# Leading slabs in eighths of the reduction, feed-forward columns by one reduction each, and three weight units without a w_ada product

## The reference

```python
mod = jax.nn.silu(c) @ w_ada + b_ada                       # 1024 x 6144
shift_m, scale_m, gate_m, shift_f, scale_f, gate_f = jnp.split(mod, 6, axis=-1)
h = rmsnorm(x, g_mix_pre) * (1.0 + scale_m[:, None]) + shift_m[:, None]
z = h @ w_in
q, k, v, fl, pu, ch, cb, cc, gl = jnp.split(z, cuts, axis=-1)
br_a = forgetting_attention(q, k, v, fl + b_f)             # softmax with a cumulated log-sigmoid of fl
...                                                        # pool mixer, short conv, gates, w_branch, w_out
x = x + gate_m[:, None] * rmsnorm(y, g_mix_post)
h2 = rmsnorm(x, g_ff_pre) * (1.0 + scale_f[:, None]) + shift_f[:, None]
y2 = jnp.square(jax.nn.relu(h2 @ w_ff1)) @ w_ff2
return x + gate_f[:, None] * rmsnorm(y2, g_ff_post)
```

## Time and profile before

| | |
|---|---|
| profiled execution | 767.74 us |
| span of its trace | 766.5 us |
| other executions | 768.32, 768.35, 767.16 us |
| PE busy | 756.8 us, 99% |
| DVE busy | 580.8 us, 76% |
| ACT busy | 447.5 us, 58% |
| POOL busy | 73.3 us, 10% |
| first product with weights | starts 14.03 us after the span's start |
| units 0 to 15 | 14.03 to 61.56 us |
| last matmul ends | about 761.3 us |

### The profile page before, as it was taken

How to read it: one execution, slowest core, us unless ns; L and a number is a source line. 1 busy time by engine, 2 the same in 40 slices (tenths; PEclk the granted TensorE clock), 3 DMA queues, 4 the chain that set the end, 5 groups by cost and what they waited for, 6 DMA issues and landing times.

```text
span 766.5 us, 11109 instructions
## 1 busy us (share of the span) xinstructions
PE 756.8 (99%) x4276; PEld 651.1 (85%) x4276; DVE 580.8 (76%) x808; ACT 447.5 (58%) x673; POOL 73.3 (10%) x128
## 2 busy tenths in 40 slices
PE   8999999999999999999999999999999999999997
PEld 6998877888898888888899997789988888888885
DVE  5989999989796576776787998667758755665664
ACT  7666687775664444444474497467547644444453
POOL 5035720000200000000020001110001100000000
PEclk9999999999999999999999999999999999999999
DMA  9989998655477776866556554446434766666641
GB/s 355 398 280 353 329 346 306 229 184 163 139 222 217 243 239 208 281 189 198 184 169 214 167 164 149 147 161 206 146 99 138 219 194 193 192 192 192 189 168 55
DMA packets 77751, 161.29 MB, mean 210 GB/s; under 512 B 5170, under 2 KB 7538, under 8 KB 77699
## 3 DMA queue, kind: packets, MB, share of 16 engines
q1 hardware_dynamic: 76272, 157.31, 62.6%
q10 hardware_dynamic: 994, 2.79, 1.0%
q0 software_dynamic: 432, 0.49, 0.2%
HBM read 159.51 MB, written 1.05 MB: 209 GB/s over the span
## 4 chain that ended last, share of the span: by engine, by line
PE 94%; DVE 3%; ACT 2%; issue 1%; DMA 0%; DVEq 0%; ACTq 0%
PE bank L2058 18%; PE bank L2059 17%; PE bank L2060 17%; PE bank L2160 15%; PE bank L2163 8%; PE bank L2134 5%; PE bank L2071 2%; PE bank L2078 2%; PE bank L2073 2%; PE bank L2518 1%; PE bank L2091 1%; PE bank L2213 1%; PE bank L2334 1%; DVE lo_ring L1123 1%; PE bank L2258 1%
## 5 line engine op out<-in xcount | busy, mean ns | idle before, releaser
L1123 DVE TENSOR_TENSOR lo_ring<-raw_ring,hi_ring 128x1024 fp32r<-128x1024 f32 x247 | 302.6, 1231 | 135.7 <-ACT hi_ring L567 134.8
L567 ACT CAST hi_ring<-raw_ring 128x1024 fp32r<-128x1024 f32 x247 | 258.5, 1052 | 233.0 <-PE bank L2060 128.3
L2058 PE MATMUL bank<-hi_ring,branch_hi 128*128 128x512 f32 x352 | 138.5, 394 | 0.0
L2059 PE MATMUL bank<-lo_ring,branch_hi 128*128 128x512 f32 x352 | 137.2, 390 | 0.0
L2060 PE MATMUL bank<-hi_ring,branch_lo 128*128 128x512 f32 x352 | 137.0, 389 | 0.0
L2160 PE MATMUL bank<-h_hi_lo,hi_ring 128*128 128x512 f32 x512 | 128.1, 392 | 0.0
L2160 PEld LDWEIGHTS bank<-h_hi_lo,hi_ring 128*128 128x128 f32 x512 | 92.9, 189 | 17.2
L2060 PEld LDWEIGHTS bank<-hi_ring,branch_lo 128*128 128x128 f32 x352 | 66.1, 188 | 14.1
L2058 PEld LDWEIGHTS bank<-hi_ring,branch_hi 128*128 128x128 f32 x352 | 66.1, 188 | 13.9 <-issue 0.9
L2059 PEld LDWEIGHTS bank<-lo_ring,branch_hi 128*128 128x128 f32 x352 | 66.2, 188 | 13.0 <-issue 0.2
L2163 PEld LDWEIGHTS bank<-h_hi_lo,lo_ring 128*128 128x128 f32 x512 | 69.8, 190 | 5.0
(11 more groups left out here) (341 smaller groups left out, 1162.8 us busy)
## 6 DMA issues: line engine op xcount, KB each, us to landing
raw_ring<-in_w_ff SPq DMA_DIRECT2D x128, 512.0 KB, 3.7
raw_ring<-in_w_in SPq DMA_DIRECT2D x63, 512.0 KB, 4.5
raw_ring<-in_w_out SPq DMA_DIRECT2D x16, 512.0 KB, 3.3
raw_ring<-in_w_xkv SPq DMA_DIRECT2D x16, 512.0 KB, 3.6
mem_v<-in_w_ada SPq DMA_DIRECT2D x13, 512.0 KB, 5.0
mem_k<-in_w_ada SPq DMA_DIRECT2D x11, 512.0 KB, 5.2
ada_ring<-in_w_ada SPq DMA_DIRECT2D x8, 512.0 KB, 7.3
raw_ring<-in_w_branch SPq DMA_DIRECT2D x8, 512.0 KB, 3.4
```

What stands on the lines that cost most here:

```text
L567: act.copy(m.hi[:, m.slot(u)], m.raw[:, m.slot(u)]).then_inc(s.hi_done, 1)
L1123: dve.tensor_tensor(m.lo[:, m.slot(u)], m.raw[:, m.slot(u)], as_f32(m.hi[:, m.slot(u)]), ALU.subtract).then_inc(s.lo_done, 1)
L2058: pe.matmul(out, a_hi, b_hi, start=start, stop=False, skip_group_check=True)
L2059: pe.matmul(out, a_hi, b_lo, start=False, stop=False, skip_group_check=True)
```

## The change

The change has three parts.

1. **Leading slabs by eighths.** Unit 2k now holds the q and k columns of the 128 rows of chunk k, unit 2k+1 their v and mixer columns. All four slabs accumulate in PSUM over k = 0 to 7 (q in banks 0 and 1, k in 2 and 3, v in 4 and 5, mixer in 6 and 7). The additions of V are gone, the copies of q, k, v and mixer out of PSUM come when each slab is complete, and the forget logits stand behind all 16 units. The host packs c as 128 x 32 (`c_blocks`); ACT takes its silu, and two DVE transposes of a broadcast operand make the row silu(c) on all partitions, in place of the matmuls of `spread_c` and two ACT passes of 128 x 1024. Both sums of squares of x are ACT's, one reciprocal root for each tile of 128 tokens is POOL's, and the transposes go tile by tile. SP issues x, two w_ada units, unit 0, and then weight and w_ada units in turn. `cumulative` on PE moves from step 1 to step 2 of `attention1`, DVE's `cum_log_f` from step 1 to step 3.
2. **Feed-forward columns.** w_ada units 24 to 39 now come transposed too, and each is one instruction of the kind of L1142 that leaves a finished column. `fold_columns`, `folded_columns`, two of the `ada_turn` and two of the `ada_sum` are gone; one small product (`ff_scale`) is added.
3. **Three units without a w_ada product.** The products stand beside the units of the list `ADA_EARLY`: 20 to 25, 27 to 30, 32 and 34 to 46.

```diff
-V_FIRST_BANK = 3
-ADA_FIRST, ADA_LATE, ADA_UNITS, ADA_RING, ADA_UNIT = 16, 40, 48, 6, 20
-FIRST_SLABS = (2, 0, 1, 3)
+X_BANKS = (7, 6, 5, 4)
+X_COPIES = (2, 3, 1)
+ADA_FIRST, ADA_COLS, ADA_LATE, ADA_UNITS, ADA_RING, ADA_UNIT = 16, 24, 40, 48, 6, 20
+
+
+ADA_EARLY = [u for u in range(ADA_UNIT, ADA_UNIT + 27) if u - ADA_UNIT not in (6, 11, 13)]
...
 def ada_at(a):
 
-    return ADA_UNIT + a - ADA_FIRST if a < ADA_LATE else FF1 + 24 + 16 * ((a - ADA_LATE) // 4) + 2 * ((a - ADA_LATE) % 4)
+    return ADA_EARLY[a - ADA_FIRST] if a < ADA_LATE else FF1 + 24 + 16 * ((a - ADA_LATE) // 4) + 2 * ((a - ADA_LATE) % 4)
...
     units = []
     w_in = t["w_in"][0]
-    columns = (0, UN, 2 * UN, 3 * NH * DH + NH)
-    units += [unit(w_in, j * UK * P, columns[i]) for j in range(RING) for i in FIRST_SLABS]
+    for k in range(KD):
+        rows = w_in[bass.ds(k * P, P), :]
+        units += [rows[:, c:c + 2 * w].rearrange("p (a n) -> p a n", n=w)[:, :, 0:UN]
+                  for c, w in ((0, UN), (2 * UN, UN + NH))]
...
-    k, c = (a - ADA_FIRST) % KD, 2 * D + (a - ADA_FIRST) // KD * D
+    if ADA_COLS <= a < ADA_LATE:
+        return t["w_ada_T"][bass.ds(2 * D + (a - ADA_COLS) * P, P), :]
...
-    for a in range(RING):
-        load_ada(a)
+    load_ada(0)
+    load_ada(1)
     for k in range(UK):
         sp.dma_start(m.raw[:, 0, k, :], units[0][:, k, :]).then_inc(s.raw_in[0] if k else s.raw_first, DMA)
-    for q in range(RING - 1):
-        u, a = RING * q, RING * q + RING
-        load(u + 1)
-        load(u + 2)
-        load_ada(a)
-        load_ada(a + 1)
-        load(u + 3)
-        load_ada(a + 2)
-        load_ada(a + 3)
-        load(u + 4)
-    for u in range(ADA_FIRST - RING + 1, UNITS):
+    for u in range(2 * KD):
+        if u:
+            load(u)
+        if u + 2 < ADA_FIRST:
+            load_ada(u + 2)
+    for u in range(2 * KD, UNITS):
...
+    act.dma_start(m.silu_block[:, :], t["c_blocks"]).then_inc(s.rows_in, DMA)
...
+    act.wait_ge(s.rows_in, DMA)
+    act.activation(m.silu_block[:, :], m.silu_block[:, :], ACT.Silu).then_inc(s.silu_ok, 1)
+    for tt in range(NT):
+        act.wait_ge(s.x_in[tt], DMA)
+        square_sum(s.xm, tt, m.x)
+    for tt in range(NT):
+        act.wait_ge(*s.xm.rstd.at(tt + 1))
+        for n in range(2):
+            cs = slice(n * UN, n * UN + UN)
             act.activation(m.norm[:, tt, cs], m.x[:, tt, cs], ACT.Copy,
                            scale=stat[:, 4 + tt:5 + tt]).then_inc(s.xm.normed.sem, 1)
 
...
-    for u in range(10, 13):
-        after(u)
-    take_half(14, 0, pair(m.qT, 0), s.q_out)
+    after(12)
+    take_half(15, 0, pair(m.qT, 0), s.q_out)
+    take_half(15, 2, pair(m.kT, 0), s.k_out)
+    act.wait_ge(s.v_ps, 1)
+    act.copy(m.v_tok[:, 0, :], bank[4][:, :]).then_inc(s.v_out, 1)
+    take_half(16, 6, pair(mix, 0), s.mixA_out)
     after(13)
...
     act.wait_ge(s.fl_ps, 1)
     act.copy(m.fl_part, bank[4][FL_LO:FL_LO + 2 * NH, 0:S]).then_inc(s.fl_sum, 1)
     after(14)
     act.wait_ge(s.fl_neg, 1)
     own.then(act.activation(m.fl_exp, m.fl_exp, ACT.Exp))
     act.activation(m.fl_exp, m.fl_exp, ACT.Ln, bias=1.0).then_inc(s.fl_ln, 1)
-    take_half(16, 6, pair(mix, 0), s.mixA_out)
...
+        if a < ADA_FIRST or ADA_COLS <= a < ADA_LATE:
+
+            if a < ADA_FIRST:
+                k, at, shift = a // 2, (KD if a % 2 == 0 else 0) + a // 2, a % 2
+            else:
+                k, at, shift = a % KD, 2 * KD + a - ADA_COLS, a < ADA_COLS + KD
+            layer = int(a >= ADA_FIRST)
+            c = B_ADA + 3 * layer * KD + k
+            dve.tensor_tensor_reduce(out=w, in0=w, in1=m.silu_ps if a < 2 else m.silu_row, scale=1.0,
+                                     scalar=cols[:, c:c + 1] if shift else m.scale_1[:, layer, k:k + 1],
+                                     op0=ALU.mult, op1=ALU.add,
+                                     accum_out=m.adacol[:, at:at + 1]).then_inc(s.ada_used, 1)
+            return
...
+    dve.wait_ge(s.silu_ok, 1)
+    for dst in (m.silu_ps, m.silu_row):
+        own.then(dve.transpose(dst.rearrange("p (j c) -> p j c", c=BLOCK),
+                               m.silu_block[:, :].unsqueeze(2).to_broadcast([P, BLOCK, BLOCK])))
     dve.wait_ge(s.cols_in, DMA)
-    own.then(dve.tensor_scalar(m.scale_1[:, :], cols[:, B_ADA + KD:B_ADA + 2 * KD], 1.0, None, ALU.add))
-    for k in range(UK):
-        ada()
-        ada()
-        mix_columns(k)
-    lo_first(0)
+    b_ada = cols[:, B_ADA:B_ADA + 6 * KD].rearrange("p (a b k) -> p a b k", a=2, k=KD)
+    own.then(dve.tensor_scalar(m.scale_1[:, :, :], b_ada[:, :, 1, :], 1.0, None, ALU.add))
+    ada()
+    mix_columns(0)
+    ada()
+    lo_half(0, 0)
     shifted_lo(s.xm, 0)
...
-    shifted_lo(s.xm, 1)
-    lo(1)
-    dve.wait_ge(s.silu_ok, 3)
-    for q in range(RING - 1):
-        u = RING * q
-        lo(u + 2)
-        for k in (UK * q + 2, UK * q + 3):
+    lo_half(0, 1)
+    ada()
+    lo_half(1, 0)
+    lo_half(1, 1)
+    mix_columns(1)
+    ada()
+    for k in range(1, KD):
+        lo(2 * k)
+        shifted_lo(s.xm, k)
+        if k < KD - 1:
             ada()
+        lo(2 * k + 1)
+        if k < KD - 1:
+            mix_columns(k + 1)
             ada()
-            mix_columns(k)
-            if k % 2 == 0:
-                lo(u + 3)
-        shifted_lo(s.xm, UK * q + 2)
-        lo(u + 4)
-        shifted_lo(s.xm, UK * q + 3)
-        lo(u + 5)
...
+    take_half(15, 1, pair(m.qT, 2), s.q_out)
+    take_half(15, 3, pair(m.kT, 2), s.k_out)
+    dve.wait_ge(s.v_ps, 1)
+    dve.tensor_copy(m.v_tok[:, 1, :], bank[5][:, :]).then_inc(s.v_out, 1)
     after(12)
-    take_half(14, 1, pair(m.qT, 2), s.q_out)
+    take_half(16, 7, pair(mix, 2), s.mixA_out)
     after(13)
-    take_half(15, 3, pair(m.kT, 2), s.k_out)
-
...
     after(14)
-    take_half(16, 7, pair(mix, 2), s.mixA_out)
...
     own.then(dve.tensor_tensor_scan(m.cum_plain, m.fl_relu, m.fl_exp, 0.0, ALU.add, ALU.add))
@@ -1410,7 +1382,7 @@
     after(15)
 
     def attention1(step):
-        if step == 1:
+        if step == 3:
             dve.wait_ge(s.cum_ps, 1)
             dve.tensor_scalar(m.cum8[:, :, :].rearrange("p a h -> p (a h)"), bank[6][:, 0:2 * NH], -1.0, None,
                               ALU.mult).then_inc(s.cum_out, 1)
...
     for j in range(RING):
+        attention1(j)
         if j == RING - 1:
             add_parts(s.mixB_part, MIX_B_BANKS, mix[:, 4:8], s.mixB_out)
-        attention1(j)
         after(MIX_B + j)
...
-            ada_turn(FF_SCALE)
-    dve.wait_ge(s.ff_cols_ps, 1)
-    folded_columns(FOLD_BANK, 0, 16, 24)
-    folded_columns(FOLD_BANK, BLOCK, 24, 32, G_FF)
+            ff_scale()
...
+    def queries_keys(u, k):
+
+        (q_hi, q_low, q_x), (k_hi, k_low, k_x) = (feature_passes(u, i, k, 2 * i) for i in range(UK))
+        if k == 0:
+            claim(0, 1)
+            q_hi()
+            q_low()
+            q_x()
+            claim(2, 3)
+            k_hi()
+            k_x()
+            k_low().then_inc(s.used, 1)
+            return
+        q_hi()
+        k_hi()
+        q_low()
+        k_low()
+        q_x()
+        k_x().then_inc(s.used, 1)
...
+    def values_mixer(u, k):
+
+        slot, outs = m.slot(u), (bank[4][:, :], bank[5][:, :])
...
+        pe.wait_ge(*ready(s.hi_done, s.hi_first, u, 0))
+        part(m.h_hi, m.hi, start=k == 0)
+        part(m.h_lo, m.hi)
+        pe.wait_ge(*ready(s.lo_done, s.lo_first, u, 0))
+        mm = part(m.h_hi, m.lo, stop=k == KD - 1)
+        if k == KD - 1:
+            mm.then_inc(s.v_ps, 1)
+        if k == 0:
+            claim(6, 7)
+        rounded, low_weights, low_features = feature_passes(u, 1, k, 6)
+        rounded()
+        low_features()
+        low_weights().then_inc(s.used, 1)
...
     def run_up(n):
 
         for _ in range(n):
-            pe.matmul(bank[5][:, 0:S], m.ones[:, :], m.x[:, 0, 0:S], start=True, stop=True)
...
+            pe.matmul(bank[0][:, 0:P], m.ones[:, :], m.ones[:, :], start=True, stop=True)
...
+    pe.wait_ge(s.ones_ok, 1)
+    run_up(13)
     turn_first()
     run_up(4)
...
+    for k in range(KD):
+        queries_keys(2 * k, k)
+        values_mixer(2 * k + 1, k)
+    free[0] = free[1] = s.q_out, 2
     free[2] = free[3] = s.k_out, 2
+    free[4] = free[5] = s.v_out, 2
+    forget_logits()
     free[6] = free[7] = s.mixA_out, 2
...
-    def fold_columns():
-
-        b = FOLD_BANK
-        claim(b)
-        ada_fold(FF_SHIFT, bank[b][:, 0:BLOCK])
-        ada_fold(FF_SCALE, bank[b][:, BLOCK:2 * BLOCK]).then_inc(s.ff_cols_ps, 1)
-        free[b] = s.ff_cols, 2
-
     def attention1(step):
-        if step == 1:
+        if step == 2:
             cumulative()
...
             mm = tile_of(tt, OUT + RING + j, UK * j, m.h_hi, m.h_lo, OUT_BANKS[1][0], j == 0, j == RING - 1)
-            if (tt, j) == (0, 1):
-                fold_columns()
```

288 lines of the change are left out of this document (94 added, 194 removed).

## The result

The changed kernel took 769.54 us (median of 7 executions, 769.07 to 772.13) against 768.32 us before (median of 7, 766.89 to 768.57). The ratio, taken from all executions, is 1.0022, 95% interval 1.0012 to 1.0031 (that of the two medians alone is 1.0016): slower by a fifth of a percent, where the prediction had said no change. The time itself lies in the predicted range, 1.3 us above the forecast, and under the 769.9 us from which the prediction would have called it slower; it is the interval that excludes no change. The profiled execution took 769.54 us with a span of 768.3, which is 1.8 us more than the one before.

What follows compares the result with a forecast made beforehand. PE, busy 99% of the span, was taken to bound the kernel. Terms -2.4 + 3.8 - 0.4 - 0.8 = +0.2 us gave 768.2 us; the forecast's own range was 766.5 to 769.1, the wider range 765.5 to 770.4.

Steps and rivals of the forecast that it cites:

- The start: Start to unit 16: first product at 11.6 us instead of 14.03, gain kept through the 16 leading units, -2.4 us.
- The wait at unit 20: Unit 20 waits for DVE's later copy out of bank 6: 2.7 to 4.0 us, taken as +3.8.
- the three operations: On DVE ahead of that copy: w_ada product, rest of unit 22, another product; 3.8 us undisturbed, 4.9 beside POOL.
- both causes that the text named: For unit 20's wait: forget logits behind unit 15 instead of ahead, and DVE's copy moved from step 1 to 3.
- The folding: Feed-forward columns near 193 us: PE's folding work of 0.36 us goes, -0.4 us.
- The wait at 127 us: PE's 0.64 us wait for DVE's rests goes with its tail, -0.8 us; rival that it stays: 769.0, chance 0.12.
- The three products: w_ada products of skipped units 26, 31 and 33 move to units 44 to 46, where DVE idles; no term.
- The falling clock: Rival, chance 0.07: PE's clock falls in unit 20's wait of 3.8 to 4 us, costing 2 us: 770.2.
- The low clock at the start: Rival, chance 0.13: PE's clock still low when the products start, 2.8 us lost over chunk 0: 771.0.

Runs made afterwards that it cites:

- the two steps moved alone: Kernel before, with only `cumulative` at step 2 on PE and DVE's copy out of bank 6 at step 3, ahead of the mixer sums: 771.59 us, ratio 1.0038.
- Without the skip: Changed kernel with the 24 w_ada products beside units 20 to 43, no unit skipped: 769.01 us, ratio 1.0008.
- the early copy: Changed kernel with DVE's copy out of bank 6 at step 2 instead of step 3: 769.11 us, ratio 1.0008.
- the early rest: Changed kernel with the last rest of the attention ahead of the rest and w_ada product of unit 46 in DVE's queue: 767.02 us, ratio 0.9989.
- the early copy and the products at units 47 to 49: Changed kernel with the copy out of bank 6 one step earlier and the three products beside units 47 to 49 instead of 44 to 46: 767.97 us, ratio 0.9990.
- one matmul in the run-up: Changed kernel with the early copy and the early rest, and one run-up matmul instead of 13 ahead of the transposes: 766.20 us, ratio 0.9972.
- the kernel without the last run-up: Changed kernel with the early copy and the early rest, without the four run-up matmuls between transposes and unit 0: 765.37 us, ratio 0.9960.
- Two exchanges of order: Changed kernel with the early copy and the early rest together: 765.22 us, ratio 0.9959.

## Why the prediction was wrong, step by step

**The start, forecast -2.4 us, measured -2.23.** Right. The first product came at 11.44 us (forecast 11.6). Chunk 0 lasted 6.07 us where the chunks behind it last 5.7; of these 0.4 us 0.15 are PE standing for chunk 1 of h, which ACT made late because it had waited for DVE's w_ada product until 16.77 us. From there to unit 16 the pace was kept; no wait on `hi_ring`, `lo_ring` or `ada_cols` above 0.2 us showed.

**The wait at unit 20, forecast +3.8 us, measured +2.62 (2.50 of it waiting).** Mechanism, line and releaser were right and the size was off, just under the 2.7 to 4.0 that the text gave. With S the start of unit 16, DVE came to the rest of unit 19 at S + 7.1 us (forecast 7.2) and to the three operations at S + 10.5 (forecast 10.7). The step that was mis-sized is the price of the three operations ahead of the copy: I took 4.9 us because POOL works in the same stretch, and they took 3.5. POOL did work there, from 66.27 us on, so the step from "POOL is under way" to "DVE is slow" is what failed here; the last section shows who was slow instead. The wait has both causes that the text named: with the copy one step earlier it is gone, and with the logits as early as before it would be about 0.8 us, by the estimate from the two steps moved alone. One reading is off, and nothing hung on it: when unit 20 began before, at 73.17 us, DVE had the whole second product ahead of it (from 73.63 us) and not half of it.

**The folding, forecast -0.4 us, measured -0.43 over the whole stretch behind unit 44.** Right as far as this stretch can tell; not tried alone.

**The wait at 127 us, forecast -0.8 us, measured -0.63.** Right. Without the skip it was there again (0.84 us), so this term belongs to the skip. Which engine PE stood for there stays open: the views name none ("issue"), before and without the skip.

**The three products, forecast nothing.** This is the step that failed: "moves three products of 1.3 to 1.8 us to units 44 to 46, where DVE has idle time". DVE did have idle time there, 1.32 us ahead of the rest at 155.83 us in the trace of before. But the idle time came *behind* the last rest of the attention and the products went *ahead* of it. I had looked at what DVE's queue has in total and not at the one operation in it that PE was about to ask for. The order on DVE would have shown it, as it had shown the copy out of bank 6: the rest L1296 behind two rests and two products. The reversal alone (last rest ahead of unit 46) took the wait away.

The sum was +0.2 us and the trace gave +1.8: 1.2 us less than forecast at unit 20, 2.5 us more at unit 44, and small terms (+0.2 each at the start and at 127 us). Two errors of opposite sign, and so luck, brought the time within 1.3 us of the forecast; that nothing would change was wrong.

**The falling clock** was a rival with 0.07, put at a wait of 4 us and at 2 us of price. The price was about right: between the two kinds of executions lie 1.97 us with the early copy (where only one stayed up), 1.7 with the early rest and 1.3 with the early copy and the products at units 47 to 49. The length of the wait was not right: the clock fell after waits of 2.2 to 2.4 us in some executions, and stayed up after waits of 2.4 and 2.5 us in others. In the changed kernel it would account for the two slowest executions, by their mean clocks.

**The low clock at the start** did not reach the products: the first four records of unit 0 last 0.71 us, and 0.72 even with one matmul in the run-up. I had taken the 13 matmuls of the run-up for 13 records of 0.24 us, 3.1 us in all. They are 26 records, as the four of before were eight, and last 5.9 us, to 0.47 us before the transposes. That they were slow is read from their durations alone, as in the earlier trace rows; the granted clock reads 1.00 in these stretches too. The same 26 records took 4.55 us in the kernel without the last run-up, with the same program up to there.

## What to carry to other kernels

Where engines run fixed queues, ask of every operation that is moved which result stands *behind* its new place and when the engine that bounds the kernel will ask for that result; idle time in the same stretch doesn't answer it. Two exchanges of order, each of one or two instructions, turned this change from 0.2% slower into 0.4% faster. And where the clock fell behind them, waits of TensorE of 2.2 to 2.4 us cost 1.6 to 1.8 times their length here.
